# The passage from attention to the output projection: low parts straight from the PSUM bank, and half of the product for two token tiles moved ahead

## The reference, cut to what matters

```python
y = jnp.concatenate([rms_norm(o_d, dsa_norm_g), rms_norm(o_f, fox_norm_g)], axis=-1)
return y @ w_out
...
x = x + g1[:, None, :] * hybrid_mixer(...)
h = modulate(rms_norm(x, norm_ffn_g[l]), sh2, sc2)
```

## Time and profile before

| | |
|---|---|
| median of 3 runs (range) | 1453.04 us (1450.92 to 1457.05) |
| profiled execution, its time / its span | 1455.72 us / 1453.9 us |
| mean granted TensorE clock | 0.982 |
| busy share of span | PE 94%, PEld 80%, DVE 69%, POOL 55%, ACT 48% |
| attention's last matmul ends | 676.8 us |
| projection begins / its tile 1 ends | 697.1 us / 719.7 us |

### The profile page before, as it was taken

The page is one execution under the profiler, slowest core; times in us unless marked ns, Lnnn a source line. Parts: engine busy times, 40 slices in busy tenths (PEclk is TensorE's granted clock), DMA queues, the critical chain, the costliest instruction groups (busy, mean ns, idle before and its releaser), DMA issues.

```text
span 1453.9 us, 20421 instructions
## 1 busy us (share of the span) xinstructions
PE 1372.5 (94%) x7099; PEld 1169.0 (80%) x7099; DVE 998.1 (69%) x1600; ACT 700.6 (48%) x1384; POOL 806.3 (55%) x531
## 2 busy tenths in 40 slices
PE   1899889999999999998999799999999999999997
PEld 0788778888799999897888588888888888788776
DVE  5743879999476778976455856666556555578697
ACT  4523345562366667676434444333333333454535
POOL 2231303324225423570002999898988885699785
PEclk9999999999999999998899899999999999999999
DMA  9121212343333867511411133333333233998864
GB/s 380 49 80 51 87 47 92 102 147 110 110 77 99 263 181 215 158 64 30 159 44 49 39 109 109 109 109 109 110 109 107 73 110 128 355 400 279 291 222 156
DMA packets 126287, 200.60 MB, mean 138 GB/s; under 512 B 10637, under 2 KB 60997, under 8 KB 125162
## 3 DMA queue, kind: packets, MB, share of 16 engines
q1 hardware_dynamic: 126186, 199.30, 41.4%
HBM read 156.99 MB, written 42.27 MB: 137 GB/s over the span
## 4 chain that ended last, share of the span: by engine, by line
PE 76%; DVE 11%; POOL 5%; issue 3%; ACT 1%; SPq 1%; DMA 1%; ACTq 0%; DVEq 0%; POOLq 0%
PE PS L2002 18%; PE PS L2003 18%; PE PS L2004 18%; PE PS L2176 8%; PE PS L2145 4%; POOL rawb L946 3%; PE PS L2163 2%; PE PS L2164 2%; POOL BS L953 2%; DVE AS L1873 1%; PE PS L2162 1%; DVE acc L1377 1%; PE PS L2206 1%; DVE junk L1708 1%; DVE PS L1925 1%
## 5 line engine op out<-in xcount | busy, mean ns | idle before, releaser
L934 POOL TENSOR_TENSOR WS<-WSf,WS 128x512 fp32r<-128x512 f32 x110 | 171.3, 1564 | 0.7 <-ACT WS L1196 0.7
L1196 ACT CAST WS<-WSf 128x512 fp32r<-128x512 f32 x110 | 68.4, 622 | 207.6 <-POOL WSf L924 206.7
L924 POOL TENSOR_TENSOR WSf<-rawg 128x512 f32<-128x512 f32 x55 | 76.7, 1394 | 160.8 <-PE PS L2004 159.7
L2176 PE MATMUL PS<-Vn,PT 128*128 128x64 f32 x1152 | 142.6, 269 | 0.0
L2002 PE MATMUL PS<-yh,WS 128*128 128x512 f32 x352 | 137.2, 390 | 2.9 <-DVE yl L1793 2.9
L2176 PEld LDWEIGHTS PS<-Vn,PT 128*128 128x128 f32 x1152 | 138.8, 192 | 0.6
L2004 PE MATMUL PS<-yh,WS 128*128 128x512 f32 x352 | 137.0, 389 | 0.0
L2003 PE MATMUL PS<-yl,WS 128*128 128x512 f32 x352 | 136.9, 389 | 0.0
L2002 PE MATMUL PS<-BS,AS 128*128 128x512 f32 x308 | 121.0, 393 | 5.8 <-DVE x1s L1957 3.0
L2003 PE MATMUL PS<-BS,AS 128*128 128x512 f32 x308 | 120.6, 391 | 0.0
L2004 PE MATMUL PS<-BS,AS 128*128 128x512 f32 x308 | 120.5, 391 | 0.0
(11 more groups left out here) (323 smaller groups left out, 3781.6 us busy)
## 6 DMA issues: line engine op xcount, KB each, us to landing
rawb<-in_w_down_dram SPq DMA_DIRECT2D x132, 256.0 KB, 4.9
rawa<-gu_scratch SPq DMA_DIRECT2D x77, 256.0 KB, 5.0
gu_scratch<-GS SPq DMA_DIRECT2D x55, 256.0 KB, 4.7
raw<-in_w_in_dram SPq DMA_DIRECT2D x24, 512.0 KB, 3.9
rawg<-in_w_gate_dram SPq DMA_DIRECT2D x22, 512.0 KB, 4.6
rawu<-in_w_up_dram SPq DMA_DIRECT2D x22, 512.0 KB, 4.3
adar<-in_ada_w_dram SPq DMA_DIRECT2D x18, 512.0 KB, 6.0
ada<-in_ada_w_dram SPq DMA_DIRECT2D x8, 1024.0 KB, 9.9
```

Of the source, the lines that this page charges most:

```text
L924: pool.tensor_tensor(WSf[m % N_SLOT][:], left(i, mat, a), left(i, mat, b), ALU.add if sign > 0 else ALU.subtract).then_inc(ws_sum, 1)
L934: pool.tensor_tensor(lo, WSf[m % N_SLOT][:] if b else left(i, mat, a), hi.bitcast(F32), ALU.subtract).then_inc(ws_ready, 1)
L2176: last = pe.matmul(PS[:, 6 + hd % 2, t * DH:(t + 1) * DH], PT[:, u % 2, j * P:(j + 1) * P], Vn[(hd // 4) % 2][:, j, cols], start=j == 0, s ...
```

## The change

- ACT makes only the high part of each group; the tile `hf2`, its 16 activations and the semaphore `yt_act` go. `roots(0)` moves from ahead of group 0 to between groups 7 and 8.
- DVE makes the low part with one `scalar_tensor_tensor` that reads the PSUM bank: bank x gain - `yh` (`y_low`). Groups 0 to 3 come right behind `normalise`, ahead of the squares; 4 and 5 behind the squares and the two small modulation operations; 6 and 7 between the first four and the last four `scaled`; 8 to 15 after them.
- A bank is now released to PE by the low part (`yt_lo`) of group g - 4.
- PE multiplies the FoX half (k = 4 to 7) of banks 0 and 1 (token tile 0) ahead of group 8, and of banks 2 and 3 (token tile 1) ahead of group 12, 24 matmuls each time. After the groups, banks 0 to 3 get only their DSA half. Tiles 2 to 7 are as before.

```diff
-            roots(0)
-
             act.wait_ge(w_ready, N_PROJ + N_OUT)
             for g, (k, half) in enumerate(Y_GROUPS):
+                if g == KT:
+                    roots(0)
                 act.wait_ge(yt_pe, g + 1)
                 act.activation(yh[:, k, cols], PS[:, 4 + g % 4, :], ACT.Identity, scale=gains[:, 1, k:k + 1]).then_inc(yt_hi, 1)
-                if g >= 2:
-                    act.wait_ge(yt_lo, g - 1)
-                act.activation(hf2[:, g % 2, :], PS[:, 4 + g % 4, :], ACT.Identity,
-                               scale=gains[:, 1, k:k + 1]).then_inc(yt_act, 1)
...
+            def y_low(g):
+                k, half = Y_GROUPS[g]
+                cols = slice(half * BANK, (half + 1) * BANK)
+                dve.wait_ge(yt_hi, g + 1)
+                dve.scalar_tensor_tensor(out=yl[:, k, cols], in0=PS[:, 4 + g % 4, :], scalar=gains[:, 1, k:k + 1],
+                                         in1=yh[:, k, cols].bitcast(F32), op0=ALU.mult, op1=ALU.subtract).then_inc(yt_lo, 1)
+
             normalise(2 * NH - 1)
+            for g in range(KT // 2):
+                y_low(g)
             dve.wait_ge(on_done, 2 * NH)
             for t in range(TT):
                 square(t, GW - LATE, LATE, (4, 0))
...
+            for g in range(KT // 2, KT // 2 + 2):
+                y_low(g)
             dve.wait_ge(yroot, 2)
             dve.reciprocal(rstd[:, 1, 0:TT], stat[:, 3, 0:TT]).then_inc(yrstd, 1)
             dve.wait_ge(yrstd, 2)
-            for t in range(TT):
+            for t in range(TT // 2):
                 scaled(t, 0)
-            for g, (k, half) in enumerate(Y_GROUPS):
-                cols = slice(half * BANK, (half + 1) * BANK)
-                dve.wait_ge(yt_act, g + 1)
-                dve.wait_ge(yt_hi, g + 1)
-                dve.tensor_tensor(yl[:, k, cols], hf2[:, g % 2, :], yh[:, k, cols].bitcast(F32), ALU.subtract).then_inc(yt_lo, 1)
+            for g in range(KT // 2 + 2, KT):
+                y_low(g)
+            for t in range(TT // 2, TT):
+                scaled(t, 0)
+            for g in range(KT, 2 * KT):
+                y_low(g)
...
+            def out_part(q, ks, first, last):
+
+                rows = slice(q // 2 * P, (q // 2 + 1) * P)
+                cols = slice(q % 2 * BANK, (q % 2 + 1) * BANK)
+                for k in ks:
+                    if q == 0:
+                        pe.wait_ge(w_ready, N_PROJ + k + 1)
+                    hi, lo = wo[k][:, 0, :], wo[k][:, 1, :]
+                    done = three(PS[:, q % 4, :], (yh[:, k, rows], yl[:, k, rows]), (hi[:, cols], lo[:, cols]),
+                                 first and k == ks[0], last and k == ks[-1])
+                    if q == 2 * TT - 1 and k in WO_LAST:
+                        done.then_inc(wo_part, 1)
+                return done
+
+            dsa_rows, fox_rows = range(KT // 2), range(KT // 2, KT)
             for g, (k, half) in enumerate(Y_GROUPS):
+                if g == KT:
+                    pe.wait_ge(yt_lo, KT // 2)
+                    for q in range(2):
+                        out_part(q, fox_rows, True, False)
+                if g == KT + KT // 2:
+                    for q in range(2, 4):
+                        out_part(q, fox_rows, True, False)
                 pe.wait_ge(yn_ok, TT if k >= KT // 2 else TT + 4 * (half + 1))
                 if g == 2:
                     pe.wait_ge(on_done, 2 * NH)
                 if g >= 4:
-                    pe.wait_ge(yt_act, g - 3)
+                    pe.wait_ge(yt_lo, g - 3)
...
                 for nh in range(2):
                     q = 2 * t + nh
-                    cols = slice(nh * BANK, (nh + 1) * BANK)
-                    if q >= 4:
+                    if q < 4:
+                        done = out_part(q, dsa_rows, False, True)
+                    else:
                         pe.wait_ge(x1_ok, q - 3)
-                    for k in range(KT):
...
+                        done = out_part(q, range(KT), True, True)
+                    done.then_inc(op_pe, 1)
```

More of the change, by code:

```diff
@@ L124 @@
 WO_HEAD = [12, 12, 13, 13, 13, 14, 14, 14]
+WO_LAST = (0, 1)
 Y_GROUPS = [(k, half) for ks in (range(KT // 2, KT), range(KT // 2)) for half in range(2) for k in ks]
@@ L340, in build @@
         wo = [at(kb, f"wo{k}", [P, 2, D], F32R) for k, kb in enumerate((104, 112, 180, 188, 196, 156, 172, 148))]
-        hf2 = at(128, "hf2", [P, 2, BANK])
         F = [at(120, "F0", [P, KT, BANK]), at(0, "F1", [P, KT, BANK])]
@@ L462, in build @@
         yt_pe = sem("yt_pe")
-        yt_act = sem("yt_act")
         yt_hi = sem("yt_hi")
@@ L2212, in turn2 @@
                 if t == 0:
-                    pe.wait_ge(yt_act, 2 * KT)
+                    pe.wait_ge(yt_lo, 2 * KT)
                 for kh in range(2):
@@ L2224, in _ @@
             for t in range(TT):
-                rows = slice(t * P, (t + 1) * P)
                 pe.wait_ge(yt_lo, 2 * KT - (4 if t < 4 else 0))
```

## The result

| | before | changed |
|---|---|---|
| median of the runs | 1455.46 us (8 runs, 1450.92 to 1462.18) | 1441.08 us (8 runs, 1439.09 to 1445.52) |
| ratio, 95% interval | | 0.9908 (0.9891 to 0.9924) |
| profiled execution: time / span | 1455.72 / 1453.9 us | 1439.96 / 1438.3 us |

The change makes the kernel faster by 0.92% (0.76 to 1.09%), some 13.4 us. The forecast was 1441.8 us, a gain of 11.25.

The account below looks back on a forecast made before the run. ACT and DVE were taken to bound the passage until 697.1 us, then PE. A 12.85 us gain less 1.6 for the clock left 11.25; off 1455.72, less 2.7 to the median, it gave 1441.8 us, range 1437.5 to 1446.7.

Parts of the forecast that it names:

- What bounds the kernel now: Between attention's end and tile 1: ACT and DVE set the pace from 676.8 to 697.1 us, PE after that.
- ACT: Transpose groups: ACT loses 16 activations of 0.57 us, a group then costs 0.57 us, and the root's 1.28 us load is hidden.
- DVE's low part: Low parts read from PSUM cost 0.65 us each, between bounds of 0.60 and 1.24 us.
- PE: Passage to tile 1 at full clock: 10.9 us moved into idle time, 1.2 earlier start, 0.8 ramp saved, together 12.85 us.
- The clock: On the first moved matmuls TensorE falls to half clock at about 681.2 us, costing 1.6 us (bounds 0 and 4.6).
- The clock holds: Rival for the passage: PE never stops over 0.3 us, so no fall; gain 12.85 us, 1440.2 us; chance 0.28.
- The median: Whole kernel: the profiled execution, 1455.72 us, lies 2.7 us above the median of 1453.04, which the forecast subtracts.
- After tile 1: Behind the passage: `xn2` has 1.3 us slack and the shift arrives whole, within 1.7 us for the feed-forward clock.
- DVE as the bound: Rival: low parts cost 1.24 us each and DVE sets the pace; gain 9.0 us, 1444.0 us; chance 0.14 including smaller waits.
- Half clock through the passage: Rival: TensorE stays at half clock for the whole passage; gain 0.3 us, 1452.7 us; chance 0.09.
- slower: Rival: short transposes mixed with matmul batches keep half clock through all 96 matmuls of two tiles; 1462 us; chance 0.04.

Follow-up runs that it names:

- either part alone: Two kernels cut from the changed one: new low parts without moved matmuls, and moved matmuls with old low parts and root order; each ratio 0.9961 to the kernel before.
- the four with fills: Profiles of the changed kernel plus extra matmuls, results overwritten, ahead of TensorE waits at the feed-forward start, in the projection stage or both; medians 1434.96 to 1441.18 us.
- only low parts: Changed kernel with the two batches of moved matmuls put back behind the groups; ratio 0.9961 to the kernel before, passage 38.12 us.
- low parts twice: Changed kernel with each of the 16 low parts computed once more into a spare tile; ratio 0.9959 to the kernel before, passage 35.49 us.
- with the root first: Changed kernel with `roots(0)` ahead of all groups again and low parts 0 to 5 behind the squares; ratio 0.9942 to the kernel before, passage 35.43 us.
- both fills again: Repeat of the changed kernel with extra matmuls at the feed-forward start and in the projection stage; 1441.18 us, ratio 0.9908 to the kernel before.
- the early fill: Changed kernel with 14 extra matmuls ahead of TensorE's wait for the forget gates' sums in the projection stage; alone 1440.21 us, ratio 0.9899 to the kernel before.

## Why the prediction was right, point by point

**What bounds the kernel now: right.** ACT at two activations a group, the root first, then PE. With either part alone the gain was only 4.7 us.

**ACT: right.** A group costs it 0.61 us (0.57 said), and the table load was hidden as said. It ended at 678.54, 0.05 us behind the sum of squares (678.49, the add behind the squares); the root was done at 678.86, and DVE asked for it only at 679.87.

**DVE's low part: right.** 0.66 us against 0.65; the near row of the same operation (0.751 us long, here 0.744) was the better guide than the dearest one (1.24). The first four `scaled` ended 10.0 us behind attention's end, as worked out (686.8 - 676.8).

**PE: right to 0.2 us.** The sum at full clock was 12.85 us, and the passage gave 12.64. The weight loads of group 8 waited 0.25 us where I had 0.1.

**The clock: wrong.** The failing step is "I expect the fall at about 681.2, on the first moved matmuls", a term of 1.6 us that measured 0 in all three profiles of the changed kernel and in the four with fills. Behind it stood the reading that transposes don't hold the clock, drawn from the time since attention's last matmul (4.4 us). The runs show another count: the clock was full under transposes for 4.5 us (only low parts) and for 7 us (low parts twice), and in this passage it fell 2 to 3 us into a real gap: PE stopped at 678.75 and it fell at 681.25 before; 675.2 and 678.1 with only the low parts; 676.9 and about 679.0 with the root first. (At the feed-forward start it was 4.05 us, from 817.15 to 821.2.) So here it was the idle time, not the kind of work, that lowered it. The rule that I cited from the Trainium skill (TensorE: Matmul & The Clock Gate, Part 4: PE-mode transpose) doesn't hold here: transposes with a single break of 0.35 us even raised the clock, at 685 us, where spaced ones at half clock had not in 15 us. The rival "The clock holds" was the true one: 12.85 off the profiled time and 2.7 to the median gave 1440.2, and 1441.08 was measured. That the forecast's 1441.8 lies just as near is luck: medians scatter by 1 to 2 us, and the term of 1.6 was wrong.

**The median.** The gain by ratio is 13.4 us (11.0 to 15.9), so 12.6 lies inside. The base had moved: 1453.04 was the median of three runs, 1455.46 that of eight.

**After tile 1: right.** `xn2` came 3.98 us behind the start of bank 1's emptying before, and here:

```profile
696.61 0.70 DVE L1811 TENSOR_TENSOR PS<-PS,g1b 128x512 f32<-128x512 f32 x1 [1.20 <-PE PS L2011]
...
699.84 0.75 DVE L1819 TENSOR_SCALAR xn<-O,rstd 128x1024 f32<-128x1024 f32 x1
```

It was ready at 700.59 and needed at 702.01: slack 1.4 (1.3 said). The shift by 12.6 us arrives at the end, plus or minus what the feed-forward start costs: in the first pair it took 2.1 us back, a little over the bound of 1.7 that I had set. The other two profiles of the changed kernel have 0.7 us back and 0.6 us gained, so it is scatter.

**DVE as the bound** was a fair rival: at the doubled price it gave 7.4 us where I had worked out 9.0. Of the 1.6 us between them the price can explain at most 16 x 0.08 = 1.3 (1.32 us a low part instead of 1.24); this was not taken apart. **Half clock through the passage** and **slower** needed a fall of the clock in the passage, and the change closes the gap in which it fell; they came in none of the seven profiles.

**Still open:** the 5 us ahead of the passage. Part of them is the clock: from 145 to 205 us it averaged 0.89 in the profile of the kernel before, 0.94 in three of the changed one and 1.00 in two with the early fill; but a third with it had 0.97 and attention's end at 674.7, no earlier than the kernels without.

## What to carry to other kernels

Write the bound engine's list with times beside it, and put ahead of each of its waits the work whose inputs are already there; then move what makes the wait end (here the root, then the low parts) so that it is done just as that work ends. Two changes on the same path need not add up, and may be worth more than their sum: freeing ACT alone left a gap, filling alone came too late, and together they gave 12.6 us where the two alone gave 9.4. Where unchanged stages differ by 5 us from run to run, measure the stage between two marks of the trace; for the changed kernel that repeated to 0.03 us.

## What the runs showed of the hardware that I had not expected

- Transposes held TensorE's clock at full (1.00 for 5 us with 1.52 us of weight loads in them, "low parts twice") and nearly unbroken ones raised it from half ("only the low parts", 680.8 to 685, one break of 0.35 us), while transposes with gaps of 0.45 us at half clock didn't (0.50 from 682 to 697).
- The same gap need not have the same end. TensorE's weight loads were idle for 3.37 us ahead of 805.95 us in the kernel before, and ahead of 796.66 with the root first, and the clock stayed full; the same 3.37 us, ahead of 788.26, 790.39 and 788.81 in the three profiles of the changed kernel, were followed by half clock from about 789.2, 790.5 and 790.0.
- The clock can stay at half with TensorE fully busy for some 17 us, at a cost of 8 us, behind a wait of 1.66 us (both fills again, 391 to 408 us).
- One extra low part per group, 0.66 us on an engine that is busy 15.3 of 20.7 us, cost 5.25 us: the busy share of VectorE told nothing of how little room it had.
